# Keys stored whole and split after they are read back; the exchange of key halves issued by ScalarE

## The reference

```
u = rms_norm(h, pre_mix_gain)
qa, ka, va, qb, kb, vb, g = split(u @ w_in)          # 16/4/4 heads of 64; 8 heads of 2 x 64; gates
qa, ka, qb, kb = rope(...)                           # x1*cos - x2*sin, x2*cos + x1*sin
o_swa  = windowed grouped attention(qa, ka, va, sink)
o_diff = (softmax(q1 k1) - lam * softmax(q2 k2)) v   # per head, then an RMSNorm of each head
merged = sigmoid(g_swa) * (o_swa @ W1) + sigmoid(g_diff) * (o_diff @ W2)
h = h + rms_norm(merged @ w_out)
```

## Time and profile before

| | us |
|---|---|
| median of three runs | 876.76 |
| lowest and highest | 876.65, 877.49 |
| the profiled execution | 876.87 |
| its span, first to last instruction | 875.1 |
| TensorE busy in it | 862.2 (99%) |
| VectorE busy | 629.0 (72%) |
| ScalarE busy | 468.0 (53%) |
| GpSimd busy | 73.7 (8%) |

### The profile page before, as it was taken

The page is one execution under the profiler, slowest core; times in us unless marked ns, Lnnn a source line. Parts: engine busy times, 40 slices in busy tenths (PEclk is TensorE's granted clock), DMA queues, the critical chain, the costliest instruction groups (busy, mean ns, idle before and its releaser), DMA issues.

```text
span 875.1 us, 13099 instructions
## 1 busy us (share of the span) xinstructions
PE 862.2 (99%) x4820; PEld 737.9 (84%) x4820; DVE 629.0 (72%) x985; ACT 468.0 (53%) x756; POOL 73.7 (8%) x96
## 2 busy tenths in 40 slices
PE   8999999999999999999999999999999999999997
PEld 6887788888888888889889888788888888888886
DVE  5867677766876666668778887888766876666665
ACT  6546534434644444444566887676653654444443
POOL 1000000000200000002322010133300100000000
PEclk9999999999999999999999999999999999999999
DMA  9955344554565555352798443755474365455531
GB/s 331 400 212 192 116 169 149 192 188 149 186 241 191 192 192 192 144 192 86 259 274 288 136 157 117 246 192 172 169 269 173 122 225 190 177 198 188 189 143 48
DMA packets 31774, 167.21 MB, mean 191 GB/s; under 512 B 4128, under 2 KB 5920, under 8 KB 14320
## 3 DMA queue, kind: packets, MB, share of 16 engines
q1 hardware_dynamic: 28992, 159.17, 51.8%
q10 hardware_dynamic: 2736, 7.42, 2.4%
HBM read 157.02 MB, written 3.83 MB: 184 GB/s over the span
## 4 chain that ended last, share of the span: by engine, by line
PE 86%; DVE 6%; ACT 3%; DMA 1%; issue 1%; POOL 1%; SPq 0%; ACTq 0%; DVEq 0%
PE ps L522 16%; PE ps L524 16%; PE ps L523 16%; PE ps L688 8%; PE ps L673 8%; PE ps L692 4%; PE ps L669 4%; PE ps L701 2%; DVE wlo L1859 2%; ACT whi L862 1%; PE ps L557 1%; PE ps L1755 1%; DMA kswap<-kraw 1%; PE ps L703 1%; PE ps L1713 1%
## 5 line engine op out<-in xcount | busy, mean ns | idle before, releaser
L1859 DVE TENSOR_TENSOR wlo<-raw,whi 128x2048 fp32r<-128x2048 f32 x134 | 307.4, 2295 | 146.3 <-ACT whi L862 145.9
L862 ACT ACTIVATE whi<-raw 128x2048 fp32r<-128x2048 f32 x134 | 256.2, 1913 | 180.0 <-PE ps L524 109.0
L522 PE MATMUL ps<-whi,xT 128*128 128x512 f32 x192 | 76.8, 400 | 0.0
L524 PE MATMUL ps<-whi,xT 128*128 128x512 f32 x192 | 75.0, 391 | 0.0
L523 PE MATMUL ps<-wlo,xT 128*128 128x512 f32 x192 | 74.8, 390 | 0.0
L1326 POOL TENSOR_TENSOR stat<-stat,cst 128x1 f32<-128x1 f32 x10 | 11.9, 1200 | 490.0 <-DVE stat L1879 261.0
L522 PE MATMUL ps<-whi,fT_h 128*128 128x512 f32 x128 | 50.2, 392 | 0.0
L523 PE MATMUL ps<-wlo,fT_h 128*128 128x512 f32 x128 | 49.8, 389 | 0.0
L524 PE MATMUL ps<-whi,fT_l 128*128 128x512 f32 x128 | 49.8, 389 | 0.0
L522 PE MATMUL ps<-x_all,whi 128*128 128x272 f32 x160 | 46.5, 291 | 1.6 <-DVE wlo L1859 1.5
L523 PE MATMUL ps<-x_all,whi 128*128 128x272 f32 x160 | 46.1, 288 | 0.0
(11 more groups left out here) (349 smaller groups left out, 1886.9 us busy)
## 6 DMA issues: line engine op xcount, KB each, us to landing
raw<-weights SPq DMA_DIRECT2D x134, 1024.0 KB, 4.8
kB<-key_parts SPq DMA_DIRECT2D x20, 272.0 KB, 3.5
kswap<-kraw SPq DMA_DIRECT2D x26, 136.0 KB, 2.5
key_parts<-knat SPq DMA_DIRECT2D x4, 544.0 KB, 7.3
cst<-consts SPq DMA_DIRECT2D x1, 1371.0 KB, 13.3
raw<-weights SPq DMA_DIRECT2D x4, 256.0 KB, 5.1
raw<-weights SPq DMA_DIRECT2D x2, 512.0 KB, 6.7
gate_a<-gain_rows ACTq DMA_DIRECT2D x2, 512.0 KB, 7.9
```

Of the source, the lines that this page charges most:

```text
L522: pe.matmul(o, lh, rh, start=first, stop=False)
L524: return pe.matmul(o, ll, rh, start=False, stop=last)
L862: act.activation(whi[s][:], raw[s][:], ACT.Copy).then_inc(split_hi, 1)
L1859: dve.tensor_tensor(wlo[s][:], raw[s][:], whi[s][:], ALU.subtract).then_inc(split_lo, 1)
```

## The change

Keys are no longer split before they are stored.

- `store_keys` now waits for `rot_ok` (VectorE has turned the keys) and stores `kswap` itself, 272 KB for a blob; `knat` and the five steps on it are gone.
- SyncE loads one head's keys (`load_keys(e)`, e = 0 to 9, two DMAs of 136 KB) into a new ring `ktwo` of two buffers. ScalarE makes the high part from there into `kB` (`keys_high(e)`) and GpSimd the rest (`keys_rest(e)`), at the slots of a new table `KEYS_AT`. TensorE waits for GpSimd's part (`kb_lo`).
- The exchange of the halves of the five key blobs is issued by ScalarE, right behind its copy to `kraw`. From blob 2 on ScalarE first waits until the store of key blob i - 2, which reads the same `kswap`, has landed (`kd_out`). The exchange for the queries stays with SyncE; the first two of them wait for a landed store as well.
- `queries_high` moves behind the softmax and the results of the units in its slot, on GpSimd the queries, keys and unit norms are issued slot by slot.
- Blob 11 now holds queries and blob 12 values (before the other way round), so the third values step moves from slot 24 to 26.
- The rows of bias for the windowed gates are loaded by SyncE at blob 22, not by ScalarE at slot 38.

```diff
-QUERIES = (6, 7, 9, 10, 12, 13, 15, 17)
+QUERIES = (6, 7, 9, 10, 11, 13, 15, 17)
-VALUES = (5, 8, 11, 14, 16)
+VALUES = (5, 8, 12, 14, 16)
-VALUES_AT = {12: 0, 18: 1, 24: 2, 30: 3, 34: 4}
+VALUES_AT = {12: 0, 18: 1, 26: 2, 30: 3, 34: 4}
+KEYS_AT = {17: 0, 19: 1, 32: 2, 38: 3, 40: 4, 42: 5, 44: 6, 46: 7, 48: 8, 50: 9}
+def stored(i):
+    return 16 * (i // 2 + 1) + (0 if i % 2 else 32)
...
@@ SyncE
             def store_keys(i):
-                sp.wait_ge(kt_ok, i + 1)
-                parts = knat[i % 2][:].bitcast(F32)
+                sp.wait_ge(rot_ok, i + 1)
+                v = kswap[i % 2]
...
+            def load_keys(e):
+                i, cc = (0, e) if e < 2 else (e // 2, e % 2)
+                if e == 0:
+                    sp.wait_ge(kd_out[0], stored(4))
+                    sp.wait_ge(kd_out[1], stored(3))
+                if e >= 2:
+                    sp.wait_ge(kb_lo, e - 1)
+                for u in range(2):
+                    v = kd[i, u::2, cc].unsqueeze(1).to_broadcast([DH, 2, KEYS])
+                    sp.dma_start(ktwo[e % 2][:, u, :], v).then_inc(ktwo_in[e % 2], 16)
...
@@ ScalarE, keys_out
+                act.wait_ge(taken_a, taken_by(16 + i))
+                if i >= 2:
+                    act.wait_ge(kd_out[b], stored(i - 2))
+                act.dma_start(kswap[b][0:DH], kraw[b][DH:P]).then_inc(ks_in[b], 16)
+                act.dma_start(kswap[b][DH:P], kraw[b][0:DH]).then_inc(ks_in[b], 16)
...
+            def keys_high(e):
+                act.wait_ge(ktwo_in[e % 2], 32 * (e // 2 + 1))
+                if e >= 2:
+                    act.wait_ge(u_sc, sets_read(e))
+                act.activation(kB[e % 2][:, :, 0, :], ktwo[e % 2][:], ACT.Copy).then_inc(kb_hi, 1)
...
-                if q in (4, 6, 8, 10, 12):
-                    keys_high(q // 2 - 2)
-                if q % 2 == 1 and (q - 5) // 2 in QUERIES:
-                    queries_high((q - 5) // 2)
```

More of the change, by code:

```diff
@@ L299, in build @@
         kswap = [new("kswap0", [P, 2, KEYS]), new("kswap1", [P, 2, KEYS])]
[L300 to L303 removed]
+        ktwo = [new("ktwo0", [P, 2, KEYS]), new("ktwo1", [P, 2, KEYS])]
+        kB = [new("kB0", [P, 2, 2, KEYS], F32R), new("kB1", [P, 2, 2, KEYS], F32R)]
         vs_meta = new("vs_meta", [P, S_KV * DH])
         o_junk = new("o_junk", [P, P])
[L306 to L307 removed]
+        rrow2 = new("rrow2", [P, TOK])
         assert top[0] <= 3 * BLOB
@@ L331, in build @@
         assert dead + KC * TOK + 2 * P <= cst_at + NCONST
-        kd = nc.dram_tensor("key_parts", (5, P, 2, 2, KEYS), F32, kind="Internal").ap()
+        kd = nc.dram_tensor("key_parts", (5, P, 2, KEYS), F32, kind="Internal").ap()
         top[0] = region + NT * D
@@ L780, in swap_halves @@
             def swap_halves(m2):
-                sp.wait_ge(taken_d if m2 in QUERIES else taken_a, taken_by(16 + m2))
+                sp.wait_ge(taken_d, taken_by(16 + m2))
                 b = m2 % 2
-                if swaps_before(m2):
-                    sp.wait_ge(kt_ok, max(SWAPPED.index(m) for m in SWAPPED if m < m2 and m % 2 == b) + 1)
+                last = max(m for m in SWAPPED if m < m2 and m % 2 == b)
+                if last in QUERIES:
+                    sp.wait_ge(kt_ok, QUERIES.index(last) + 1)
+                else:
+                    sp.wait_ge(kd_out[b], stored(last))
                 sp.dma_start(kswap[b][0:DH], kraw[b][DH:P]).then_inc(ks_in[b], 16)
@@ L834, in _ @@
                     store_keys(m - 6)
-                if m in (12, 13):
-                    load_shared_keys(m - 12)
-                if m == 19:
-                    load_keys(0)
-                if 22 <= m < 29:
-                    load_keys(m - 21)
+                if 12 <= m < 16:
+                    load_keys(m - 12)
+                if 22 <= m < 28:
+                    load_keys(m - 18)
+                if m == 22:
+                    sp.wait_ge(u_sc, S_UNITS)
+                    for t in range(NT):
+                        sp.dma_start(gate_s[:, t, :], grow[5].partition_broadcast(P)).then_inc(bias_in[2], 16)
                 if m - 7 in QUERIES:
                     store_queries(m - 7)
-                if m - 4 in SWAPPED:
+                if m - 4 in QUERIES:
                     swap_halves(m - 4)
@@ L1205, in _ @@
                                    ACT.Copy, scale=subgain[:]).then_inc(d_hi, 1)
-                if q == 38:
-                    act.wait_ge(u_sc, S_UNITS)
-                    bias_rows(2, gate_s)
+                if q % 2 == 1 and (q - 5) // 2 in QUERIES:
+                    queries_high((q - 5) // 2)
+                if q in KEYS_AT:
+                    keys_high(KEYS_AT[q])
                 if q == 54:
@@ L1366, in _, with keys_rest @@
                                    ALU.subtract).then_inc(kt_ok, 1)
-            for U in range(S_UNITS, UNITS):
-                pool.wait_ge(d_o, U - S_UNITS + 1)
-                st = ostat[:, U % 3]
-                link(pool, "pool", rsqrt(st[:, 2:3], st[:, 1:2], st[:, 0:1], 1.0 / P))
-                pool.tensor_scalar(o_tok[U % 3][:], o_tok[U % 3][:], st[:, 2:3], None, ALU.mult).then_inc(d_n, 1)
+            def keys_rest(e):
+                pool.wait_ge(kb_hi, e + 1)
+                pool.tensor_tensor(kB[e % 2][:, :, 1, :], ktwo[e % 2][:], kB[e % 2][:, :, 0, :],
+                                   ALU.subtract).then_inc(kb_lo, 1)
+            for q in range(2 * OUT2):
+                if q % 2 == 1 and (q - 5) // 2 in QUERIES:
+                    queries_rest((q - 5) // 2)
+                if q in KEYS_AT:
+                    keys_rest(KEYS_AT[q])
+                U = q - U0 - 3
+                if S_UNITS <= U < UNITS:
+                    pool.wait_ge(d_o, U - S_UNITS + 1)
+                    st = ostat[:, U % 3]
+                    link(pool, "pool", rsqrt(st[:, 2:3], st[:, 1:2], st[:, 0:1], 1.0 / P))
+                    pool.tensor_scalar(o_tok[U % 3][:], o_tok[U % 3][:], st[:, 2:3], None, ALU.mult).then_inc(d_n, 1)
             for t in range(NT):
```

68 lines of the change are left out of this document (22 added, 46 removed).

## The result

The changed kernel takes 891.14 us in the median of six runs (889.28 to 893.39), against 876.7 for the kernel before (876.05 to 877.49). The ratio is 1.0166, with an interval of 1.0147 to 1.0186: it is slower by 14 us, and outside the range that was forecast. The profiled execution is one of the longer ones, 893.32 us with a span of 891.5, 16.4 above the span of before.

A forecast was written before the change was run, and what follows sets the result against it. TensorE, busy 862.2 of 875.1 us, was taken as the bound. Terms +0.2 (to slot 18) - 0.2 - 0.6 + 1.1 - 0.3 + 0.1 = +0.3 on 876.87 gave 877.2 us, 8-in-10 range 873.8 to 880.6.

The forecast's parts named there:

- Blob 5: TensorE's wait ahead of blob 5: exchange of blob 2 lands at 423.1, weights ready at 427.5, 1.5 us saved.
- Blob 7: Restart ahead of blob 7: exchange of blob 4 lands in 3.0 us, restart at 441.0 not 443.64, 2.6 us ahead so far.
- The crowd stays: Rival, chance 0.25: exchange of blob 4 lands after 6.1 us as before, slot 18's transposes wait until 461.4, 880.3 us.
- Slot 18: Added wait at slot 18's transposes: keys land at 457.0, start at 458.3, earlier gain given back, net +0.2 us.
- The rule on issuing engines: Skill's rule, used for the slow side: all engines' DMAs share 16 engines, so ScalarE's exchange is no faster; 880.3 us.
- The units: Terms behind slot 18: slot 24 -0.2, slot 30 -0.6, slot 26 +1.1, slot 40 -0.3, added key steps +0.1 us.
- Slots 30 and 40: TensorE's waits there: slot 30's 0.58 goes, -0.6 us; slot 40's shrinks, -0.3 of 0.79 us.
- Slot 26: Copy of the values comes behind slot 25's `queries_high`, at 488.0, TensorE wants it at 486.9: +1.1 us, 0 to 1.9.
- The ten key steps: Key splitting on ScalarE and GpSimd, in slots 38 to 50 ahead of `hi`: +0.1 us, from 0 to +1.5.
- The rival on the other side: Chance 0.25: `ktwo` lands within 4 us of issue, slot 18 starts by 456.0, 2.1 us gain stays, 874.9 us.
- the gain of 2.6 us up to blob 7: Up to blob 7's restart, 441.0 instead of 443.64; 0 if the exchange of blob 4 takes 6.1 us to land.
- bound of any gain: TensorE's waits between 396 and 660 us, 4.6 us or 0.53% of the time, as the most the change can win.

The follow-up runs named there:

- the best one: Changed kernel with turned keys in own buffers, first two key sets split in slots 20 and 21, old roles of blobs 11 and 12: 872.32 us, ratio 0.9955.
- the last kernel of the experiments: Changed kernel with own buffers for turned keys, late first key sets, old roles of blobs 11 and 12, key exchanges issued by SyncE: 872.34 us, ratio 0.9951.

## Why the prediction was wrong

**The picture was right, the sizes were not.** The prediction had the chain link by link: exchange 2, `lo` of blob 5, store 2 behind a load, exchange 4, `lo` of blob 7, the last store, the exchange of blob 6, `ktwo`, the copy. Each of its end points against what the trace shows, and what the link itself added:

| link | predicted | measured | off by this link |
|---|---|---|---|
| exchange 2 issued | 420.1 | 420.5 | 0.4 |
| its landing | 423.1 | 426.4 | 2.9 |
| `lo` of blob 5 | 427.5 | 430.7 | -0.1 |
| store 2 landed | 433.0 | 436.8 | 0.6 |
| exchange 4 landed | 436.6 | 443.9 | 3.5 |
| `lo` of blob 7 | 441.0 | 448.3 | 0 |
| last store landed | 447.0 | 454.5 | 0.2 |
| first `ktwo` issued | 450.7 | 458.2 | 0 |
| `ktwo` landed | 457.0 | 467.4 | 2.9 |
| transposes of slot 18 | 458.3 | 468.7 | 0 |

The steps of the engines behind a landing came out within 0.1 us. Three landings carry 9.3 of the 10.4 us: the two exchanges and `ktwo`. **The failed step is the price of these three landings**, taken as 2.5, 3.0 and 6.3 us for transfers that had a load of 1 MB close ahead of them; they took 5.4, 6.5 and 9.2 (`ktwo` counted from its first issue).

- *Blob 5, "It lands by the median of 2.5":* it took 5.4 behind its second issue. The median is that of exchanges which SyncE issues ahead of the load of its slot. On ScalarE's queue, and started later by its store, this one came 1.3 us behind a load of 1 MB. The prediction had the order of the two issues wrong: it said that the exchange of blob 2 would go at 420.1 and never asked what SyncE does at 419. The earlier trace rows had the right size, 6.1, for a small transfer behind a load.
- *Blob 7, "I take 3.0":* 6.5. Its upper bound, 6.1 by the earlier trace rows, was named and put aside because "only one load and a half-sized store are on the way". These were enough. Half of "The crowd stays" came true with this, but even its 880.3 was far too low, since it let only this one landing be late.
- *Slot 18, "457.0, 6.3 after their issue":* the last of the pair landed 8.6 us after its own issue, within the bound of 8.7 that the prediction kept. It also read the earlier trace rows wrongly there: the 8.7 belong to the second load, issued at 453.8, so it landed 1.3 us behind blob 12 and not 0.3, which is 1.0 of the 2.9 us. It was taken as its own case, though it too stands close behind loads, issued at 455.73 and 457.56. That this is the cause is argued from neighbours and not tested: the first half of `ktwo` took 7.1 us here and 6.9 in the kernel with SyncE as issuer, where the two loads ahead were 1.8 us apart, and 5.8 and 4.7 where they were 3.6 and 4.0 apart (the kernel that holds back two loads, and the best one). **The three bounds are not independent:** their upper ends came together, and the range held only one at a time. With the 6.1 of the earlier trace rows for both exchanges and its own 8.7 for `ktwo`, the sum of this part would have come out 3.6 + 3.1 + 2.4 = 9.1 us later.
- *The rule on issuing engines* (the Trainium skill, DMA: Bandwidth & Descriptors, "Issuing engines are not separate DMA queues") agrees with the trace: 876.99 against 876.54 us with the issuer exchanged, and 2.4 against 6.5 us by what was issued ahead on another queue. It belonged in the first term, blob 5, and not in a rival alone.

**The clock was missing.** No term, rival or bound of the prediction knew that a wait costs more than its length. The granted clock was 1.00 in every row that it had. Behind slot 18 this is 2.2 us by the kernels with filler matmuls. Behind slot 26 it is another 1.5: from the scores of slot 25 to those of slot 26 the changed kernel takes 9.1 us, the one with own buffers, whose clock stayed at 1.00 after the same wait, 7.6. A reader of the Trainium skill had the warning (TensorE: Matmul & The Clock Gate, "HAM oscillation — how this bites in real kernels": waits for data throw the array back to its slow level, and what follows starts slow). The trace agrees in kind: 0.50, 0.51 and 0.53 behind three waits.

**The units.** *Slots 30 and 40* lost their waits: -0.8 and -1.0 by the starts, where -0.6 and -0.3 were put down. *Slot 26, "+1.1, from 0 to 1.9":* 2.0 and the clock behind it. The mechanism was right. The size was off because the scaling on ScalarE began 0.5 us before TensorE wanted the values, not 1.6 before (485.3 against 486.9). *The ten key steps, "+0.1, from 0 to +1.5":* 1.8, over the upper bound, and on a path that the prediction did not name: it looked for the delay in `hi`, `lo` and the softmax, and it came by way of GpSimd's norm of the results. The sum of this part, +0.1, is 5.8 in the trace, of which 2.4 are the clock behind slot 18.

**The rival on the other side** was of the right sign and the right place, at a chance of 0.25. What made the forecast "no change" was the gain of 2.6 us up to blob 7 that was to pay for the rest. That gain needed both exchanges to land short, and keeping it needed a short landing of `ktwo`.

**Why the change itself isn't bad.** With the turned keys in their own buffers, the key steps behind the values, and blob 11 giving values, the same idea (keys stored whole, split from the ring's copy) takes 872.32 us, 4.2 under the kernel before in that comparison. In this pair of profiles TensorE is 6.4 us ahead of the kernel before at slot 45, 5.9 of them won from 396 us on, and the key steps give 1.8 back; the spans are 870.5 and 875.1. So the prediction's "bound of any gain", 4.6 us of idle time in brackets, was too low.

## What to carry to other kernels

A wait for a landed DMA in front of another DMA makes a chain in which landings add up; filling TensorE's waits did not move it (468.99 against 468.74). Before a transfer is put behind a store because both share a buffer, look for a second buffer; here that was worth 12.6 us. When a transfer moves to another queue, write down what each other queue issues in the three us ahead of it and right behind it, and take its landing from rows with the same neighbours, not from the median of all. Where several terms hang on the same unknown, move them together in the range. And a new wait on the engine that bounds the kernel can cost, beside its length, a stretch at the lower clock; where a later wait for DMAs sets the timing anyway, as here ahead of slot 18, that stretch costs nothing.

## What the runs showed of the hardware

- An exchange (two halves of 136 KB) lands by how close a load of 1 MB stands to it. In the changed kernel its halves took 2.3 and 2.4 us with the last load 7.5 us back (426.64), and 4.9 to 6.5 us where one was issued 1.4 to 2.5 us ahead from the other engine's queue. In the best kernel, 3.0 us behind a load, it was 3.5 us for both halves (421.79). On SyncE's own queue, 1.8 us behind a load, it was 5.1 us (421.30, the last kernel of the experiments).
- To be issued just ahead is not enough: the exchange of blob 0 went at 403.95 and 404.54, the load at 404.07, and it took 6.0 and 5.9 us; in the kernel before, with the load 1.2 us behind its first half (403.86), 2.3 and 2.4.
- TensorE's granted clock fell to 0.50 to 0.53 behind idle stretches of 3.19, 5.69 and 1.84 us of the changed kernel, and not behind its 2.58 us ahead of blob 7. The length of the wait alone does not tell. Nine kernels wait 1.84 to 1.92 us in slot 26: behind it the clock was 0.53 to 0.61 over three us in five of them, and 1.00 in four, among them the one with own buffers (the stretch of 489 to 492 us). Behind the 4.45 us of that kernel's slot 18 it was 0.66 over five us. What decides was not found.

```profile
458.00:463.00 5.00, 5.00 (x23) 4.17 (x22) 2.29 (x1) 4.02 (x8) 2.02 (x3) 0.66 0.04 17
489.00:492.00 3.00, 3.00 (x29) 2.54 (x30) 2.93 (x5) 1.72 (x8) 1.00 (x1) 1.00 0.57 233
```

- Waits ahead of blobs 5 and 7 differed by up to 2 us between two kernels that are alike up to there, the changed one and the one with fillers in slot 18 alone (3.19 and 3.65, 2.58 and 4.58). What sets that was not followed up.
